# One expert row in four summed on ScalarE and GpSimd instead of TensorE

## The reference

```python
def peer_ffn(h, w_pq, peer_keys, peer_u, peer_v):
    ...
    best, pos = lax.top_k(cand, PEER_TOPK)
    experts = jnp.take_along_axis(cand_ix, pos, axis=-1)
    gates = jax.nn.softmax(best, axis=-1).astype(h.dtype)
    ...
    def block(args):
        tb, eb, gb = args
        act = jax.nn.gelu(jnp.einsum('nd,nhkd->nhk', tb, peer_u[eb]))
        return jnp.einsum('nhk,nhkd->nd', gb * act, peer_v[eb])
```

## Time and profile before

| | |
|---|---|
| median of 2 runs | 5211.5 us (5204.42 to 5218.58) |
| profiled execution, span | 5217.8 us |
| PE busy | 4403.5 us, 84% |
| DVE busy | 3444.6 us, 66% |
| POOL busy | 1498.3 us, 29% |
| ACT busy | 1436.0 us, 28% |
| gathers (software queue) | 1342.26 MB |
| all DMA, mean | 284 GB/s |

### The profile page before, as it was taken

The page is one execution under the profiler, slowest core; times in us unless marked ns, Lnnn a source line. Parts: engine busy times, 40 slices in busy tenths (PEclk is TensorE's granted clock), DMA queues, the critical chain, the costliest instruction groups (busy, mean ns, idle before and its releaser), DMA issues. The chain is left out here.

```text
span 5217.8 us, 51329 instructions
## 1 busy us (share of the span) xinstructions
PE 4403.5 (84%) x14836; PEld 2229.8 (43%) x14836; DVE 3444.6 (66%) x9196; ACT 1436.0 (28%) x4114; POOL 1498.3 (29%) x1410
## 2 busy tenths in 40 slices
PE   7999898888878878887788998988988788897776
PEld 3588665433323323322235886654333233332222
DVE  5555565667676777777565555746677767777775
ACT  2211342222222222222222113522222222222222
POOL 0122100333343434433301220004333334344432
PEclk9988899999999999999999888999999999999999
DMA  7100102899999999999870001019999999999997
GB/s 258 39 3 1 48 1 73 365 418 415 406 416 405 414 420 401 415 419 415 344 258 17 3 1 48 1 73 416 420 414 411 420 404 414 410 405 420 420 414 311
DMA packets 243939, 1481.06 MB, mean 284 GB/s; under 512 B 26384, under 2 KB 32144, under 8 KB 79296
## 3 DMA queue, kind: packets, MB, share of 16 engines
q0 software_dynamic: 184320, 1342.26, 62.5%
q1 hardware_dynamic: 59264, 135.37, 7.2%
q10 hardware_dynamic: 64, 0.07, 0.0%
HBM read 1473.96 MB, written 3.64 MB: 283 GB/s over the span
## 5 line engine op out<-in xcount | busy, mean ns | idle before, releaser
L1646 PE MATMUL psall<-left,diag 128*128 128x512 f32 x2848 | 1373.0, 613 | 323.3 <-ACT diag L1541 322.8
L1646 PE MATMUL psall<-right,diag 128*128 128x512 f32 x2272 | 1105.0, 617 | 265.7 <-ACT diag L1541 265.6
L1379 POOL DMA_INDIRECT left<-in_peer_uv,eidx x712 | 735.8, 1033 | 1797.3 <-PE psall L1646 1058.3
L1464 DVE CUSTOM_DVE_ANT_0 left<-left,mixed 128x1024 f32<-128x1024 f32 x712 | 873.2, 1226 | 543.1 <-DMA left<-in_peer_uv,eidx 543.1
L1646 PEld LDWEIGHTS psall<-left,diag 128*128 128x128 f32 x2848 | 500.1, 190 | 1163.8 <-ACT diag L1541 721.2
L1464 DVE CUSTOM_DVE_ANT_0 right<-right,mixed 128x1024 f32<-128x1024 f32 x568 | 696.8, 1227 | 422.3 <-DMA right<-in_peer_uv,eidx 422.3
L1548 ACT ACTIVATE act<-dot 128x1 f32<-128x1 f32 x1280 | 259.5, 203 | 2411.7 <-DVE dot L1464 2410.7
L1379 POOL DMA_INDIRECT right<-in_peer_uv,eidx x568 | 587.4, 1034 | 884.8 <-PE psall L1646 861.5
L1646 PEld LDWEIGHTS psall<-right,diag 128*128 128x128 f32 x2272 | 401.2, 191 | 945.3 <-ACT diag L1541 597.6
L1541 ACT ACTIVATE diag<-cons,wgt 128x128 f32<-128x128 f32 x1280 | 493.8, 386 | 2.3 <-issue 0.3
L498 POOL TENSOR_TENSOR mlt<-lt,lmask 128x512 f32<-128x512 f32 x120 | 173.0, 1452 | 535.6 <-DVE lt L596 370.8
(11 more groups left out here) (289 smaller groups left out, 5106.5 us busy)
## 6 DMA issues: line engine op xcount, KB each, us to landing
wlate<-in_w_mod SPq DMA_DIRECT2D x32, 1024.0 KB, 5.3
wq<-in_w_pq SPq DMA_DIRECT2D x64, 512.0 KB, 7.9
left<-in_peer_uv,eidx POOLq DMA_INDIRECT x712, 15.9
right<-in_peer_uv,eidx POOLq DMA_INDIRECT x568, 15.9
w<-in_w_mod SPq DMA_DIRECT2D x4, 2048.0 KB, 10.8
wtm<-in_w_mod SPq DMA_DIRECT2D x4, 2048.0 KB, 18.0
wtm<-in_w_in_tm SPq DMA_DIRECT2D x4, 2048.0 KB, 9.0
right<-in_w_out SPq DMA_DIRECT2D x4, 2048.0 KB, 11.4
```

The lines of the kernel that those rows point to most:

```text
L1379: nc.gpsimd.indirect_dma_start(out=p.slots[n % SLOT], out_offset=None, in_=d["peer_uv"], in_offset=bass.IndirectOffsetOnAxis(ap=p.eidx[:, ...
L1464: nc.vector.tensor_tensor_reduce(out=u_row, in0=u_row, in1=p.mixed[:, t, :], scale=1.0, scalar=0.0, op0=ALU.mult, op1=ALU.add, accum_out=p ...
L1646: mm = nc.tensor.matmul(bank, p.diag[:, n % DIAGS, :], p.slots[n % SLOT][:, D + 512 * c:D + 512 * c + 512], start=(s == 0), stop=(s == UNI ...
```

## The change

Of each four rows the last (n % 4 = 3) no longer goes to PE. ACT scales its v by the weights in its own slot, and POOL adds the slot to a sum `acc` in SBUF; the first such row of a unit is copied to `acc` instead. The slot is freed by POOL's instruction. In POOL's stream the addition of row n stands behind the issue of gather n+6 (`BACK`). The other three rows go to PE as before, with four `diag` buffers in place of eight. `add_unit` adds `acc` to each bank, then multiplies by `gt2` (a new instruction of 1024 columns, which signals `pool_read`), then adds to `x`. The sum `acc` takes 4 KB per partition, and four `diag` buffers give back 2 KB.

```diff
--- before.py
+++ after.py
@@ -64,7 +64,9 @@
 UNIT = 2 * TOPK
 MARKS = 18
 SLOT = 9
-DIAGS = 8
+DIAGS = 4
+EACH = 4
+BACK = 6
 WR = 4
 SUBS = 5
 
@@ -1205,6 +1207,21 @@
                 own.mark(nc.vector.tensor_tensor(x, x, bc(p.gsub[:, :], 1, 4), ALU.mult))
 
 
+def summed_by_pool(n):
+
+    return n % EACH == EACH - 1
+
+
+def pool_rows(n):
+
+    return n // EACH
+
+
+def pe_rows(n):
+
+    return n - n // EACH
+
+
 def unit_of(u):
 
     return (0, u) if u < C else (1 + (u - C) % (NT - 1), (u - C) // (NT - 1))
@@ -1355,7 +1372,7 @@
                 if i >= WR:
                     sp.wait_ge(sem("pq_mm"), i - WR + 1)
                 if i == 6 * C:
-                    sp.wait_ge(sem("y_read"), 2 * C)
+                    sp.wait_ge(sem("pool_read"), C)
                     spread(sp, p.gt2, d["mid_rows"][3][1:2, :], "load_gt2s")
                 sp.dma_start(p.wq[:, i % WR, :, :], d["w_pq"][bass.ds(lay, 1), i % (4 * C)].rearrange("l p k n -> p (l k) n")
                              ).then_inc(sem(f"load_q{i % WR}"), 16)
@@ -1366,6 +1383,19 @@
 
         @block.gpsimd
         def _(pool):
+            def add_row(n):
+
+                i = pool_rows(n)
+                pool.wait_ge(sem("scaled_rows"), i + 1)
+                v_row = p.slots[n % SLOT][:, D:2 * D]
+                if n % UNIT == EACH - 1:
+                    if n > UNIT:
+                        pool.wait_ge(sem("pool_read"), n // UNIT)
+                    nc.gpsimd.tensor_copy(p.acc[:, :], v_row).then_inc(sem("pool_sum"), 1)
+                else:
+                    pool.wait_ge(sem("pool_sum"), i)
+                    nc.gpsimd.tensor_tensor(p.acc[:, :], p.acc[:, :], v_row, ALU.add).then_inc(sem("pool_sum"), 1)
+
             for n in range(ROWS):
                 t, col = place(n)
                 if n % TOPK == 0:
@@ -1374,11 +1404,18 @@
                     pool.wait_ge(sem("wout_mm"), 2 * NT)
                 if n == 5:
                     pool.wait_ge(sem("h2_ready"), NT)
-                if n >= SLOT:
-                    pool.wait_ge(sem("row_free"), n - SLOT + 1)
+                if n >= SLOT and summed_by_pool(n - SLOT):
+                    pool.wait_ge(sem("pool_sum"), pool_rows(n - SLOT + 1))
+                elif n >= SLOT:
+                    pool.wait_ge(sem("row_free"), pe_rows(n - SLOT + 1))
                 nc.gpsimd.indirect_dma_start(out=p.slots[n % SLOT], out_offset=None, in_=d["peer_uv"],
                                              in_offset=bass.IndirectOffsetOnAxis(ap=p.eidx[:, t, col:col + 1], axis=0)
                                              ).then_inc(sem(f"row_in{n % SLOT}"), 16)
+                if n >= BACK and summed_by_pool(n - BACK):
+                    add_row(n - BACK)
+            for n in range(ROWS - BACK, ROWS):
+                if summed_by_pool(n):
+                    add_row(n)
 
         @block.vector
         def _(dve):
@@ -1435,15 +1472,18 @@
 
                 t, col = place(n)
                 dve.wait_ge(sem("gelus"), n + 1)
-                if n >= 16:
-                    dve.wait_ge(sem("diags"), n - 15)
+                if n >= 16 and summed_by_pool(n - 16):
+                    dve.wait_ge(sem("scaled_rows"), pool_rows(n - 15))
+                elif n >= 16:
+                    dve.wait_ge(sem("diags"), pe_rows(n - 15))
                 nc.vector.tensor_tensor(p.wgt[:, n % 16:n % 16 + 1], p.act2[:, n % 16:n % 16 + 1], p.gat[:, t, col:col + 1],
                                         ALU.mult).then_inc(sem("weights"), 1)
 
             def add_unit(u):
 
                 t, _ = unit_of(u)
-                dve.wait_ge(sem("row_free"), UNIT * (u + 1))
+                dve.wait_ge(sem("row_free"), pe_rows(UNIT * (u + 1)))
+                dve.wait_ge(sem("pool_sum"), pool_rows(UNIT * (u + 1)))
                 if u == 0:
                     dve.wait_ge(sem("load_gt2"), 16)
                 if u == C:
@@ -1452,8 +1492,10 @@
                     cols = slice(c * 512, c * 512 + 512)
                     if u >= 1:
                         dve.wait_ge(sem("residual"), u)
-                    nc.vector.tensor_tensor(p.y[:, cols], bank, p.gt2[:, cols], ALU.mult).then_inc(sem("y_read"), 1)
+                    nc.vector.tensor_tensor(p.y[:, cols], bank, p.acc[:, cols], ALU.add).then_inc(sem("y_read"), 1)
                 dve.wait_ge(sem("y_read"), 2 * u + 2)
+                nc.vector.tensor_tensor(p.y[:, :], p.y[:, :], p.gt2, ALU.mult).then_inc(sem("pool_read"), 1)
+                dve.wait_ge(sem("pool_read"), u + 1)
                 nc.vector.tensor_tensor(p.x[:, t, :], p.x[:, t, :], p.y[:, :], ALU.add).then_inc(sem("residual"), 1)
 
             for n in range(ROWS):
@@ -1536,9 +1578,14 @@
             def diag_of(n):
 
                 act.wait_ge(sem("weights"), n + 1)
-                if n >= DIAGS:
-                    act.wait_ge(sem("row_free"), n - DIAGS + 1)
-                nc.scalar.activation(p.diag[:, n % DIAGS, :], p.ident, ACT.Copy, scale=p.wgt[:, n % 16:n % 16 + 1]).then_inc(sem("diags"), 1)
+                if summed_by_pool(n):
+                    v_row = p.slots[n % SLOT][:, D:2 * D]
+                    nc.scalar.activation(v_row, v_row, ACT.Copy, scale=p.wgt[:, n % 16:n % 16 + 1]).then_inc(sem("scaled_rows"), 1)
+                    return
+                i = pe_rows(n)
+                if i >= DIAGS:
+                    act.wait_ge(sem("row_free"), i - DIAGS + 1)
+                nc.scalar.activation(p.diag[:, i % DIAGS, :], p.ident, ACT.Copy, scale=p.wgt[:, n % 16:n % 16 + 1]).then_inc(sem("diags"), 1)
 
             j = len(early)
             for n in range(ROWS):
@@ -1639,12 +1686,15 @@
                 while j < len(steps) and before_row[j] <= n:
                     step(j)
                     j += 1
+                if summed_by_pool(n):
+                    continue
                 if s == 0 and u >= 2:
                     pe.wait_ge(sem("y_read"), 2 * (u - 1))
-                pe.wait_ge(sem("diags"), n + 1)
+                i = pe_rows(n)
+                pe.wait_ge(sem("diags"), i + 1)
                 for c, bank in enumerate(sum_banks(u)):
-                    mm = nc.tensor.matmul(bank, p.diag[:, n % DIAGS, :], p.slots[n % SLOT][:, D + 512 * c:D + 512 * c + 512],
-                                          start=(s == 0), stop=(s == UNIT - 1))
+                    mm = nc.tensor.matmul(bank, p.diag[:, i % DIAGS, :], p.slots[n % SLOT][:, D + 512 * c:D + 512 * c + 512],
+                                          start=(s == 0), stop=(s == UNIT - 2))
                 mm.then_inc(sem("row_free"), 1)
 
 
@@ -1830,6 +1880,7 @@
             p.mixedT = [p.h2T[:, 4 * (t // 4):4 * (t // 4) + 4, P + t % 4 * P:2 * P + t % 4 * P] for t in range(NT)]
             p.diag = sb(c1, "diag", [P, DIAGS, P])
             p.y = p.junk
+            p.acc = sb(c1, "acc", [P, D])
             p.r_top = sb(c1, "r_top", [P, 2, TOPK])
             p.r_ix = sb(c1, "r_ix", [P, 2, TOPK], U32)
             p.r_ixf = sb(c1, "r_ixf", [P, 2, TOPK])
```

## The result

| | before | change |
|---|---|---|
| median | 5211.5 us | 5506.8 us (5501.6 to 5512.0, 2 runs) |
| profiled execution, span | 5217.8 us | 5510.2 us |
| PE / DVE / POOL / ACT busy, share of the span | 84 / 66 / 29 / 28% | 75 / 73 / 47 / 31% |
| DMA, mean | 284 GB/s | 269 GB/s |

The ratio is 1.0566 [1.0542, 1.059]: slower by 5.7%, 295 us. The forecast was 5545 us.

A forecast was written before the change was run, and what follows sets the result against it. The prediction took the gather to bound the expert rows. The profiled span of 5217.8 us plus 312 (wait), 20 (adds) and 2 (layer ends) gave 5552, or 5545 us against the median; range 5400 to 5710.

The forecast's parts named there:

- What bounds the kernel: Expert rows: bound by the gather at 411 GB/s, 2.49 us a row; relieving PE costed at nothing.
- The wait in add_unit: A unit's first POOL copy waits for `pool_read`, the gathers drain: 8.2 us lost per unit, 38 times, 312 us.
- to the release of the copy: After row 32u+8 lands: dot to first add 1.63 us, two adds 1.31, new product 1.22; 4.2 us.
- DVE's add to `x` first, and the copy: Both start together and one waits; DVE taken as first, ending at 5.4 us, then the copy at 1.4 us.
- gap, issue to the dot of row 32u+10: After the copy: 0.3 us between instructions, then 6.1 us to landing, as the second layer's first gather took.
- the ends of the layers: End of each layer some 1 us longer from scaling, POOL's add and the new product; 2 us in both layers.
- POOL's wait: At the copy behind gather 32u+9, POOL issues nothing for 20 us, copy included, and the nine gathers drain.
- the 7.65 us that was hidden: In one place of the kernel before POOL waited 7.65 us, and the landings behind it kept their cadence.
- POOL's adds: 140 adds a layer of 128x1024, 2.5 us each, fitting in each four rows; 20 us allowed, ends 0 and 40.
- The rule from L600: A DVE instruction with two SBUF inputs waits until POOL's has ended; L600, a 128x512 product, takes 1.64 us.
- The rival in which this makes DVE the bound: Between bubbles, adds of 3.2 us or handovers make cycles 10.5 us: 140 to 280 us more, 5685 to 5825; chance 17%.
- The clock: Rival: PE idles in the bubbles and drops to 1.2 GHz, up to 600 us, 5800; chance 4%.

The follow-up runs named there:

- e4: e1 with POOL's adds and copies cut to one column from the third unit on, the rest of that output left out: 5212.7 us, 0.9998 of the kernel before.
- e8: Kernel before, every fourth gather from row 19 on fetching 4 KB per token in place of 8, without v: 4837.7 us, 0.9277.
- e1: The change with two sums in turn, so the copy need not wait for the add_unit before it: 5219.4 us, 1.0017 of the kernel before.
- e2: The change with add_unit behind the dot of row 32u+6 instead of 32u+8: 5322.4 us.
- e7: The change with BACK = 8 for 6, so two more gathers are out when POOL stops: 5328.2 us, 1.0214.
- e9: The change with add_unit behind the dot of row 32u+4 instead of 32u+8, single sum: 5224.8 us, 1.0018 of the kernel before.
- e5: Kernel before plus one 128x1024 POOL addition into idle memory behind every fourth gather from row 61 on, sum unused: 5222.1 us, 1.0018.
- e3: The change with add_unit behind the dot of row 32u+9 instead of 32u+8: 5558.7 us.

## Why the prediction was right

**What bounds the kernel.** Right, by e4 and e8.

**The wait in add_unit.** Right in its place, its count and nearly in its size; e1, e2, e7 and e9 take it away or shrink it as forecast. Its terms, for the unit shown above, counted from the dot of row 32u+8:

| term | forecast | measured |
|---|---|---|
| to the release of the copy | 4.2 us | 4.3 us |
| DVE's add to `x` first, and the copy | 2.6 us | 2.0 us |
| gap, issue to the dot of row 32u+10 | 0.3 + 6.1 us | 0.2 + 6.5 us |
| less two rows | 5.0 us | 5.0 us |
| lost in the hole | 8.2 us | 8.0 us |

The copy is shorter than I took it: 1.03 us alone for my 1.4. DVE did come first, as I let it, by 0.1 us. The issue behind the copy is longer, 1.75 us for 0.94, with a dot beside it. The two misses offset each other, and that is luck.

**Where the 38 us between 5545 and 5507 lie.** By e1 the wait is worth 287 us and not 312, 25 us less, and all the rest 8 to 9 us and not 22, 13 us less. The wait first. The sum above counts the hole against two rows of 2.49 us. In the kernel before, the landings of rows 32u+8 and 32u+10 are 5.2 us apart in the mean of units 1 to 18, with some of SP's loads between; in the change they are 12.9 apart (28 of 36 units, the trace lacks a landing in the others). That is 7.7 us lost. The next two rows take 0.35 us more than before, and the other 28 of the unit 0.7 us less, 71.2 for 71.9, which makes the 7.4 us of the whole. Why these 28 come sooner is not shown; a little of SP's loads now falls into the hole, 0.18 MB in these two rows for 0.09. Of the 281 us by which the stretches from row 40 to row 639 of both layers grew, 260 are the time in which the gather's queue moves no packet.

The rest was put at 20 us for the adds and 2 us for the ends of the layers. e5 has the adds at some 9 us. From the last dot of a layer to its last addition to `x` it takes 9.6 and 8.6 us, 6.9 in both before: 2.7 and 1.7 us more, where I had 1.

**POOL's wait** was put at 20 us with the copy in it and is 14.9 us with it, 12.9 without, in the mean. The size was wrong. POOL is later with gather 32u+9 than I had it, and its own adds stand ahead of that gather; the line of gathers gives 10.3 us from issue to landing in the median for the 15.9 of the earlier trace rows, 4.1 rows in flight in the place of 6.4. It made no difference, as the hole's end is set by the release and not by the start of the wait. A bound that compares waits alone, 20 us with the 7.65 us that was hidden, would have misled: 7.6 us cost 112 us in e2. The right measure is the rows in flight at the release.

**POOL's adds.** 2.34 us undisturbed for the 2.5 of my estimate, 3.3 us in the median, which is above the 3.2 us that I named for the rival below: an add that starts while a dot runs lasts that much longer. The rule from L600 held, but the one that waits behind the add is mostly the weighing, not the dot:

```profile
1299.06 1.23 DVE L1506 CUSTOM_DVE_ANT_0 left<-left,mixed 128x1024 f32<-128x1024 f32 x1 [1.01 <-DMA left<-in_peer_uv,eidx]
1299.16 3.33 POOL L1397 TENSOR_TENSOR acc<-acc,left 128x1024 f32<-128x1024 f32 x1 [0.55 <-ACT left L1583]
...
1300.21 2.29 DVE L1479 TENSOR_TENSOR wgt<-act,gat 128x1 f32<-128x1 f32 x1
```

The rival in which this makes DVE the bound is refuted by e1: DVE is busy 89% of the window there, and the DMA share is 1.00. In the change itself the share is 1.01 between the holes, with the adds at 3.3 us.

**The clock.** The granted clock fell from 0.99 to 0.84 and 0.85 in the expert windows, and the mean of the sums' matmuls rose from 613 (L1646) to 724 ns (L1696), both for `left`. So PE's total fell by 247 us and not by the 600 that I named as a sign, and PE is busy 69% of the window, not below 65%: both signs missed, as they were worked out without a lower clock. It cost no time that the runs can tell: the clock is 0.88 in the expert window of e1 and 0.90 in that of e4, and both are within 0.2% of the kernel before. In the change itself the transfers between the holes are full at 0.86. As a rival it is refuted. In the unit above PE idles from 1332.84 to 1335.36 us, and the clock in the window of 1336 to 1338 is 0.50, the level of 1.2 GHz. The Trainium skill (TensorE: Matmul & The Clock Gate, Part 1) says that the clock halves after idling, and this window agrees.

**The pages weighed.** The Trainium skill (GPSIMD Engine Reference, 4.1, Engine selection) has GpSimd near line rate for one input, and this was the better price: 1.03 us for 1024 columns. The fixed 2.0 us besides the transfer (the Trainium skill, DMA: Bandwidth & Descriptors, anatomy of one DMA) gave the estimate of about 4.5 us, and it was too short here: 6.2 us is the shortest landing of a gather in the change, and 6.5 us the one behind the copy. Here the measured row decides.

## What to carry to other kernels

Look at where a wait stands in the stream of the engine that also feeds the bound. POOL's adds were affordable; one wait between two gathers, for a thing that another engine does only eight rows into the unit, made nearly all of the loss. Count the transfers that are in flight when the release comes, and move either side of the wait until they cover it: here two rows earlier on one engine were worth the same as two more issues on the other. And an engine that waits for the bound has nothing to give: taking a quarter of PE's matmuls away changed the time by nothing.

## What the runs showed of the hardware

- A gather's issue on POOL takes 0.93 us at least. One that starts while DVE's dot (two SBUF inputs) runs ends some 0.8 us after the dot: 1.58 us at 1317.66 and 1.75 us at 1333.86 in the change, against 0.97 us behind the copy of e3, where no dot runs.
- From the start of that issue to the first packet of the gather it takes 2.45 us in the change and 1.68 us in e3, both the median of 38: the longer issue delays the transfer by as much.
- An instruction of one column can take as long as its neighbour on the other engine: POOL's copy of one column 1.17 us beside DVE's addition to `x` of 1.23 us, DVE's weighing 2.3 us beside POOL's add, 0.15 us alone.
- POOL adds 128x1024 in float32 with two inputs in 2.34 us and copies as much in 1.03 us, when nothing is in the way.
